# A transformer layer with expert retrieval in fp32: 160 instead of 144 tokens by gathered rows, low halves on GpSimd, rotary scores in fp32r

## The chip, the core and the metric

One core of a Trainium2 chip runs the whole layer. The metric is device time in microseconds (us) of one execution, lower is better; the time given is the median of several runs. The engines are PE (TensorE matmul), PEld (its weight loads), DVE (VectorE), ACT (ScalarE), POOL (GpSimd) and SP (SyncE, which only issues DMAs).

## What is computed

512 tokens of width 2048 go through latent attention (8 heads, 128 plain and 64 rotary columns), a gating unit, an output projection, a retrieval over 16384 one-neuron experts, a per-layer gate and a last RMSNorm. The part that takes most of the time is the retrieval:

```
q  = a @ w_q ; s1, s2 = scores against two sets of 128 keys, per head
experts, gates = the best 16 of the pair sums, per token and head (8 heads: 128 picks per token)
h   = sum over d of u_exp[experts] * a
out = sum over picks of gates * gelu(h) * v_exp[experts]
```

Rotary attention adds `q_rope . k_rope` (64 columns) to `q_nope . k_nope` (128 columns) before the softmax.

## The kernel before

Activations lie transposed, channels on partitions and tokens along the free axis. Large products are made of three fp32r matmuls each (`three`): an fp32 number is split into a high half (a copy rounded to fp32r) and a low half (the number minus its high half), and high by high, high by low and low by high are added in PSUM. Weights come in tiles of 1 MB through a stream of slots. For slot n, SP loads `raw`, ACT writes `wH` (L588), DVE writes `wL` = raw - wH (L986, called `lo`), and PE multiplies. SP, ACT, DVE, POOL and PE each work through a fixed list in order and wait on semaphores, so whatever stands behind a waiting instruction in the same list waits as well.

The retrieval serves two sets of tokens in two ways.

**Dense columns.** The first 368 tokens (`TD`) are multiplied with all 16384 experts. In the u stretch 128 slots ("chunks" of 128 experts) give the neurons' inputs: 16 products of `three`, 48 matmuls of 368 columns in each. 32 of these slots lie in the routing of the heads (with 16 slots of 512 columns for the queries), 96 follow. In the v stretch 128 slots of 48 matmuls go back to the 2048 channels. In v slot v (v = 8g+q) the chunk v+8 is got ready: SP loads `pre_in` and `gate_in`, POOL multiplies them (L551), ACT makes the high half `actH` (L841, `weight_hi`), DVE the low half `actL` (L1502, `weight_lo`); PE reads both from the next group of eight slots on.

**Gathered tokens.** The last 128 tokens stand one on a partition. For each of their 128 picks POOL gathers a row of u and v per partition (L543, 16 KB by 128 partitions, 2.1 MB), DVE makes the dot product (`dot`, L1476), ACT gelu and gate (`weigh_pick`, L858 and L862), DVE adds the weighted v row (`add_row`, L1485). 16 more tokens (`BT`) are spread over 8 sets of partitions, so that all their 128 picks take `B_PICKS` = 16 further gathers: 144 in all. A pick is two steps, dot and add. 60 picks are dealt over the chunks 36 to 118 of the u stretch on three row buffers (between two gathers POOL scatters gates with four indirect DMAs, L524), 4 over the last eight chunks on one buffer, and 80 over 118 v slots (`v_step`), on the two row buffers `rows3` and `rows4`. The gather of pick j+2 waits for the add of pick j.

In a v slot the lists read:

- ACT: `wH` of the next slot; for each dot of this slot `weigh_pick`; then `weight_hi`.
- DVE: accumulate; the slot's first step; `lo` of the next slot; its second step, if any; accumulate; `weight_lo`.
- POOL: multiply chunk v+8; then, for each add of this slot, the gather of two picks on.

The retrieval's last part and the rest of the layer stay on PE too. In the attention, 32 items (8 heads by 4 query blocks) each take an fp32 matmul over the plain columns (L1840), an fp32 matmul over the 64 rotary columns (L1841), a mask matmul (L1842), transposes and the product with the values.

Of the kernel before, what the change touches and what calls it, by code (L numbers as in the profile page):

```python
# [35 lines left out]
BT = 16  # L36
# [4 lines left out]
PARTS = SETS // HEADS  # L41
A_PICKS = HEADS * TOPK
B_PICKS = TOPK // PARTS
# [109 lines left out]
def trunk_layer(nc, a, stream, out, gates_dram, pre_dram):  # L153
# [22 lines left out]

    aH = at("aH", [KD, T], R, A0)
# [72 lines left out]
    gates_b = at("gates_b", [B_PICKS], F, C0 + 12 * KB + 640)  # L250
    dots_b = at("dots_b", [B_PICKS], F, C0 + 12 * KB + 704)
    pick_wb = at("pick_wb", [B_PICKS], F, C0 + 12 * KB + 768)
# [4 lines left out]
    pick_w = at("pick_w", [P], F, C0 + 13 * KB + 512)  # L257
    ones = at("ones", [P], F, C0 + 14 * KB)
# [12 lines left out]
    with ctx:  # L271
        ps = ctx.enter_context(nc.psum_tensor("ps", [P, 8, 512], F))

        def sem(name):
            return ctx.enter_context(nc.semaphore(name))
# [19 lines left out]
        kv_copied = sem("kv_copied")  # L295
        score_done, nbias_ready, exp_done, p_ready = sem("score_done"), sem("nbias_ready"), sem("exp_done"), sem("p_ready")
# [59 lines left out]
        def _(sp):  # L356
# [104 lines left out]
        def _(pool):  # L461
# [43 lines left out]
            for i in range(4):  # L505
                pool.dma_start(hT[:, 4 * i:4 * i + 4, :], a["x"][:, 4 * i:4 * i + 4, :]).then_inc(x_again, 16)
# [68 lines left out]
        def _(act):  # L575
# [398 lines left out]
        def _(dve):  # L974
# [242 lines left out]
            for n in range(ITEMS + 1):  # L1217
# [8 lines left out]
                if n >= 1:  # L1226
# [5 lines left out]
                    V.tensor_scalar(prob[m % 2][:, 0:w], prob[m % 2][:, 0:w], rinv[:, m:m + 1], None, ALU.mult).then_inc(p_ready, 1)  # L1232
                if n >= NT + 4 and n % NT == 0 or n == ITEMS:
# [275 lines left out]
            for c in range(ROUTE_U + 2, KEYS):  # L1509
                scale_chunk(c - 1, (c - 1) % 2, CUM[nu + c - 1])  # L1510
                steps = range(u_step(c), u_step(c + 1))
                for o in steps[0:1]:
                    pick_step(o)
# [3 lines left out]
                if c >= KEYS - GROUP:  # L1517
                    weight_lo(c - KEYS + GROUP, c - KEYS + GROUP, 0, pre_in[c % 2])
# [10 lines left out]
            def v_end(g, q, b, m, i):  # L1529
                c = GROUP * (g + 1) + q  # L1530
# [3 lines left out]
                weight_lo(c, q, 1 - b, pre_in[q % 2])  # L1534
# [124 lines left out]
        def _(pe):  # L1659
# [168 lines left out]
            pe.wait_ge(rope_ready, 5)  # L1828
            pe.wait_ge(mean_ready, NORMS["sgu"] + 1)
            ITEMS = HEADS * NT  # L1830
            for n in range(ITEMS + 3):
                if n < ITEMS:
# [5 lines left out]
                    r = slice(64 * (h % 2), 64 * (h % 2) + 64)  # L1838
# [279 lines left out]
```

## Time and profile before

| | us |
|---|---|
| median of 3 runs | 3081.89 (3081.18 to 3085.0) |
| profiled execution | 3090.69 |
| its span | 3089.0 |

The span was profiled once; 1.7 us of the profiled execution lie outside it. On the page PE is busy for 3052.4 us (99%), DVE for 2228.9 (72%), ACT for 1061.4 (34%), POOL for 1211.7 (39%). A PE row's length holds the pipeline's depth and says little of its rate: the distance from one start to the next is the rate. Of the 40 slices of the span, the DMA engines are at 9 tenths or more in most of those from 1080 to 2780 us.

### The profile page before, as it was taken

How to read it: one execution, taken by the hardware profiler on the slowest of the kernel's cores; microseconds unless marked ns; L12 is line 12 of the kernel's file. 1: busy time of each engine (PE TensorE's matmuls, PEld its weight loads, DVE VectorE, ACT ScalarE, POOL GpSimd, SP SyncE). 2: the span in 40 equal slices, each digit the busy share in tenths (PEclk: the TensorE clock that was granted, in tenths of full speed). 3: DMA queues.
4: the chain of work that ended last, by engine and by line, in shares of the span. 5: the costliest groups of instructions: out<-in, count | busy, mean ns of one | idle time of the engine just before them, and what ended most of it. 6: DMA issues, size and time to landing. Idle time of an engine off the chain costs nothing. (4 is left out here: it accounts for less than half of the span.)

```text
span 3089.0 us, 42590 instructions
## 1 busy us (share of the span) xinstructions
PE 3052.4 (99%) x16888; PEld 2862.8 (93%) x16888; DVE 2228.9 (72%) x2944; ACT 1061.4 (34%) x1328; POOL 1211.7 (39%) x702
## 2 busy tenths in 40 slices
PE   9999999999999999999999999999999999999998
PEld 7888668899999999999999999999999999999887
DVE  5465553478778767777777658888888888997545
ACT  5234442333332433333333333333333333334422
POOL 1010000008888888788887112332333232440000
PEclk9999899999999999999999999999999999999999
DMA  8472202235545599999999779989889999994222
GB/s 296 165 245 90 96 36 101 95 119 126 136 119 137 128 359 347 337 352 347 357 313 373 269 298 356 356 356 361 352 348 360 358 356 366 350 347 162 96 95 95
DMA packets 191487, 768.59 MB, mean 249 GB/s; under 512 B 68608, under 2 KB 121872, under 8 KB 129392
## 3 DMA queue, kind: packets, MB, share of 16 engines
q1 hardware_dynamic: 90768, 407.45, 36.0%
q0 software_dynamic: 81632, 335.12, 30.3%
q10 hardware_dynamic: 18944, 24.14, 2.3%
q8 instruction: 85, 1.39, 0.2%
q14 instruction: 58, 0.48, 0.0%
HBM read 714.00 MB, written 52.62 MB: 248 GB/s over the span
## 5 line engine op out<-in xcount | busy, mean ns | idle before, releaser
L1664 PE MATMUL ps<-aH,wH 128*128 128x368 f32 (+2 forms) x3088 | 1076.2, 349 | 7.5 <-DVE wL L986 5.4
L1665 PE MATMUL ps<-aL,wH 128*128 128x368 f32 (+2 forms) x3088 | 1072.3, 347 | 0.0
L1666 PE MATMUL ps<-aH,wL 128*128 128x368 f32 (+2 forms) x3088 | 1072.2, 347 | 0.0
L588 ACT ACTIVATE wH<-raw 128x2048 fp32r<-128x2048 f32 x333 | 637.9, 1915 | 1013.3 <-PE ps L1666 845.9
L986 DVE TENSOR_TENSOR wL<-raw,wH 128x2048 fp32r<-128x2048 f32 x333 | 783.8, 2354 | 193.2 <-ACT wH L588 192.3
L524 POOL DMA_INDIRECT gates<-gates_r,idx_d x384 | 746.8, 1945 | 369.6 <-DVE gates_r L1387 237.6
L1664 PE MATMUL ps<-actH,wH 128*128 128x368 f32 x2048 | 673.6, 329 | 3.3 <-DVE wL L986 3.3
L1665 PE MATMUL ps<-actL,wH 128*128 128x368 f32 x2048 | 673.5, 329 | 0.0
L1666 PE MATMUL ps<-actH,wL 128*128 128x368 f32 x2048 | 673.5, 329 | 0.0
L1664 PEld LDWEIGHTS ps<-aH,wH 128*128 128x128 f32 x3088 | 580.7, 188 | 47.3 <-DVE wL L986 6.4
L1665 PEld LDWEIGHTS ps<-aL,wH 128*128 128x128 f32 x3088 | 580.8, 188 | 38.7 <-issue 1.0
L1666 PEld LDWEIGHTS ps<-aH,wL 128*128 128x128 f32 x3088 | 580.7, 188 | 38.5
L1664 PEld LDWEIGHTS ps<-actH,wH 128*128 128x128 f32 x2048 | 384.7, 188 | 3.6 <-DVE wL L986 3.6
L1666 PEld LDWEIGHTS ps<-actH,wL 128*128 128x128 f32 x2048 | 384.7, 188 | 0.0
L1665 PEld LDWEIGHTS ps<-actL,wH 128*128 128x128 f32 x2048 | 384.6, 188 | 0.0
L551 POOL TENSOR_TENSOR pre_in<-pre_in,gate_in 128x368 f32<-128x368 f32 x128 | 184.6, 1442 | 413.1 <-DMA gate_in<-gates 410.9
L543 POOL DMA_INDIRECT rows<-uv_rows,idx_s x128 | 214.7, 1677 | 335.5 <-DVE hT L1485 296.2
L1476 DVE SCALAR_TENSOR_TENSOR rows<-rows,ps 128x2048 f32<-128x2048 f32 x128 | 291.7, 2279 | 19.3 <-DMA rows<-uv_rows,idx_s 18.9
L1485 DVE SCALAR_TENSOR_TENSOR hT<-rows,pick_w,hT 128x2048 f32<-128x2048 f32 x128 | 300.2, 2346 | 0.0
L1396 DVE TENSOR_TENSOR ut<-ps,rstd 128x368 f32<-128x368 f32 x128 | 69.2, 541 | 211.8 <-PE ps L1666 188.2
L1507 DVE TENSOR_TENSOR hT<-hT,ps 128x368 f32<-128x368 f32 x256 | 135.5, 531 | 89.1 <-PE ps L1666 88.5
L858 ACT ACTIVATE dots<-dots 128x1 f32<-128x1 f32 x128 | 26.0, 203 | 259.2 <-DVE rows L1476 244.0
(260 smaller groups left out, 1981.2 us busy)
## 6 DMA issues: line engine op xcount, KB each, us to landing
raw<-s_pu SPq DMA_DIRECT2D x128, 1024.0 KB
raw<-s_pv SPq DMA_DIRECT2D x128, 1024.0 KB
gates<-zeros POOLq DMA_DIRECT2D x23, 1024.0 KB, 8.3
pre<-ut ACTq DMA_DIRECT2D x128, 184.0 KB
pre_in<-pre SPq DMA_DIRECT2D x128, 184.0 KB
gate_in<-gates SPq DMA_DIRECT2D x128, 184.0 KB
raw<-s_out SPq DMA_DIRECT2D x16, 1024.0 KB
raw<-s_pq SPq DMA_DIRECT2D x16, 1024.0 KB
```

The lines of the kernel that those rows point to most:

```text
L524: pool.indirect_dma_start(out=gates_flat, out_offset=bass.IndirectOffsetOnAxis(ap=idx_d[0:m, t, c:c + 1], axis=0), in_=gates_r[0:m, t, c:c ...
L543: pool.indirect_dma_start(out=rows[ROW_AT[j]][:, :, :].rearrange("p a d -> p (a d)"), out_offset=None, in_=a["uv_rows"], in_offset=bass.In ...
L551: nc.gpsimd.tensor_tensor(pre_in[b][:, :], pre_in[b][:, :], gate_in[b][:, :], ALU.mult).then_inc(act_gated, 1)
L588: A(wH[parity][:, :], raw[at_n][:, :], ACT.Copy).then_inc(hi_ready, 1)
L986: V.tensor_tensor(wL[parity][:, :], src[:, :], wH[parity][:, :].bitcast(F), ALU.subtract).then_inc(lo_ready, 1)
L1396: V.tensor_tensor(ut[b][:, :], ps[:, 6 + b, 0:TD], rstd[:, 0:TD], ALU.mult).then_inc(chunk_scaled, 1)
L1476: V.scalar_tensor_tensor(r3, r3, 1.0, act_of, ALU.mult, ALU.mult, accum_out=d).then_inc(dot_done, 1)
L1485: V.scalar_tensor_tensor(hT[:, :, TA:T], v3, pick_w[:, j:j + 1], hT[:, :, TA:T], ALU.mult, ALU.add).then_inc(pick_done, 1)
L1507: V.tensor_tensor(h, h, ps[:, 4 + k % 4, 0:TD], ALU.add).then_inc(h_acc, 1)
L1664: mm(out, wh, xh, start=start, stop=False)
L1665: mm(out, wh, xl, start=False, stop=False)
L1666: return mm(out, wl, xh, start=False, stop=stop)
```

## The change

- `BT` goes from 16 to 32: 160 tokens are gathered and 352 columns stay dense (`TD`). The 32 tokens lie in 4 sets, which take `B_PICKS` = 32 gathers: 160 picks, of which 96 are dealt over the same 118 v slots.
- The low half of the activations, `actL`, is made by POOL, in `apply_gates` behind its multiply and behind a wait for ACT's high half, and no longer by DVE. POOL's gathers stand behind it.
- In the last eight chunks of the u stretch, ACT makes the high half before it weighs a pick, and each of the four last picks gets its dot in one slot and its add in the next.
- SP loads late chunk 2 before value tiles 4 to 6.
- The rotary parts of q and k are split in high and low halves (`ropeQ`, `ropeKH`, `ropeKL`; ACT copies, DVE subtracts), and the rotary scores are two fp32r matmuls: one over 128 rows (q high and q low against k high, doubled) and one over 64 rows (q high against k low). The product of low by low is left out. Eight DVE scalings of `mixT` move into the attention's items, and three of four reloads of x wait for the last score.

```diff
-BT = 16
+BT = 32
 SETS = P // BT
-PARTS = SETS // HEADS
-B_PICKS = TOPK // PARTS
+B_PICKS = A_PICKS // SETS
...
     if c > KEYS - GROUP:
-        return 2 * (U_PICKS - LATE + min((c - KEYS + GROUP + 1) // 2, LATE))
+        return 2 * (U_PICKS - LATE) + min(c - KEYS + GROUP, 2 * LATE)
...
             load_late_chunk(1)
+            load_late_chunk(2)
             load_value(4)
             load_value(5)
-            for v in range(2, KEYS - GROUP):
+            load_value(6)
+            for v in range(3, KEYS - GROUP):
...
                 nc.gpsimd.tensor_tensor(pre_in[b][:, :], pre_in[b][:, :], gate_in[b][:, :], ALU.mult).then_inc(act_gated, 1)
+                pool.wait_ge(act_whi, c + 1)
+                nc.gpsimd.tensor_tensor(actL[c // GROUP % 2][:, c % GROUP, 0:TD], pre_in[b][:, :],
+                                        actH[c // GROUP % 2][:, c % GROUP, 0:TD].bitcast(F), ALU.subtract).then_inc(act_wlo, 1)
...
+                    if s == 1:
+                        r = head_rows(m)
+                        act.wait_ge(rope_ready, 2 + m // 2)
+                        A(ropeQ[r, m, :], qT[r, 8 + m // 2, :], ACT.Copy).then_inc(rope_hi, 1)
...
                 u_beat(c, c % 2, nu + c, 0)
+                weight_hi(c - KEYS + GROUP, c - KEYS + GROUP, 0, pre_in[c % 2])
                 for o in range(u_step(c), u_step(c + 1)):
                     if o % 2 == 0:
                         weigh_pick(o // 2)
-                weight_hi(c - KEYS + GROUP, c - KEYS + GROUP, 0, pre_in[c % 2])
...
+                if 5 <= n + 4 < HEADS:
+                    rope_low(n + 4)
+                if 0 <= n - 10 < SGU_TILES:
+                    g = n - 10
+                    V.scalar_tensor_tensor(mixT[:, 8 + g, :], mixT[:, 8 + g, :], gain("sgu", g), rstdB[:, :],
+                                           ALU.mult, ALU.mult).then_inc(sgu_scaled, 1)
...
-            def weight_lo(c, j, b, src):
-                dve.wait_ge(act_whi, c + 1)
-                V.tensor_tensor(actL[b][:, j, 0:TD], src[:, :], actH[b][:, j, 0:TD].bitcast(F), ALU.subtract).then_inc(act_wlo, 1)
...
-                weight_lo(c, q, 1 - b, pre_in[q % 2])
...
-                    mm(o, qT[r, 8 + h // 2, t], krT[r, 0:w], start=False, stop=False)
+                    if qt == 0:
+                        pe.wait_ge(rope_lo, 2 + h)
+                    mm(o, ropeQ[:, h, t], ropeKH[:, 0:w], start=False, stop=False)
+                    mm(o, ropeQ[r, h, t], ropeKL[r, 0:w], start=False, stop=False)
```

POOL's list in the v stretch, before (`pre_in` is the multiply, `rows` a gather):

```order
L551 TENSOR_TENSOR pre_in_132<-pre_in_132,gate_in_134 128x368
L543 DMA rows_86<-uv_rows,idx_s 128x4096
L551 TENSOR_TENSOR pre_in_131<-pre_in_131,gate_in_133 128x368
L543 DMA rows_87<-uv_rows,idx_s 128x4096
L551 TENSOR_TENSOR pre_in_132<-pre_in_132,gate_in_134 128x368
```

and of the change:

```order
L561 TENSOR_TENSOR pre_in_134<-pre_in_134,gate_in_136 128x352
L563 TENSOR_TENSOR actL_85<-pre_in_134,actH_83 128x352
L553 DMA rows_90<-uv_rows,idx_s 128x4096
L561 TENSOR_TENSOR pre_in_135<-pre_in_135,gate_in_137 128x352
L563 TENSOR_TENSOR actL_85<-pre_in_135,actH_83 128x352
L553 DMA rows_89<-uv_rows,idx_s 128x4096
```

The subtraction that reads `actH` has come between each multiply and the gather behind it. On ACT, in the same place of the change, the instruction that writes `actH` stands behind the weighing of the slot's dot, as it did before:

```order
L601 ACTIVATE wH_71<-raw_69 128x2048
L879 ACTIVATE dots<-dots 128x1
L883 ACTIVATE pick_w<-dots,gates_r 128x1
L862 ACTIVATE actH_83<-pre_in_135 128x352
L601 ACTIVATE wH_72<-raw_70 128x2048
```

Nothing moved on ACT there. What is new is that POOL now waits for the fourth row. On PE, the first two items of the attention before:

```order
L1840 MATMUL ps<-kT,qT 128x128
L1841 MATMUL ps<-krT,qT 128x128
L1842 MATMUL ps<-causalR,identR 128x128
L1840 MATMUL ps<-kT,qT 128x256
L1841 MATMUL ps<-krT,qT 128x256
```

and of the change:

```order
L1868 MATMUL ps<-kT,qT 128x128
L1871 MATMUL ps<-ropeKH,ropeQ 128x128
L1872 MATMUL ps<-ropeKL,ropeQ 128x128
L1873 MATMUL ps<-causalR,identR 128x128
L1868 MATMUL ps<-kT,qT 128x256
L1871 MATMUL ps<-ropeKH,ropeQ 128x256
L1872 MATMUL ps<-ropeKL,ropeQ 128x256
```

Each rotary matmul has become two, of another type.

## Rows read from the trace of the kernel before

**Rows 1.** Windows: busy us (x instructions) by engine, PE clock, DMA share, GB/s.
```profile
700.00:1000.00 300.00, 300.00 (x1657) 281.25 (x1657) 245.21 (x778) 96.88 (x97) 258.07 (x127) 1.00 0.51 130
1100.00:1700.00 600.00, 600.00 (x3602) 600.00 (x3601) 451.31 (x315) 201.47 (x260) 487.24 (x269) 1.00 0.98 348
1800.00:1880.00 80.00, 72.20 (x412) 71.29 (x411) 50.38 (x41) 26.98 (x32) 15.98 (x13) 0.96 0.79 308
1880.00:2700.00 820.00, 820.00 (x4922) 820.00 (x4921) 712.22 (x620) 273.12 (x343) 273.03 (x173) 1.00 0.91 356
```

**Rows 2.** Timeline of PE (start, us, operation): 512 columns, then 368 columns.
```profile
307.93 0.39 PE L1666 MATMUL ps<-cqH,wL 128*128 128x512 f32 x1
...
308.61 0.39 PE L1666 MATMUL ps<-cqH,wL 128*128 128x512 f32 x1
...
1499.92 0.33 PE L1664 MATMUL ps<-aH,wH 128*128 128x368 f32 x1
...
1501.92 0.33 PE L1664 MATMUL ps<-aH,wH 128*128 128x368 f32 x1
```

**Rows 3.** Groups by line and form: the 368 column matmuls of u and of v.
```profile
L1664 PE MATMUL ps<-aH,wH 128*128 128x368 f32 x2048 | 675.2, 330 | 4.5 <-DVE wL L986 4.5
L1664 PE MATMUL ps<-actH,wH 128*128 128x368 f32 x2048 | 673.6, 329 | 3.3 <-DVE wL L986 3.3
```

**Rows 4.** Timeline of the attention on PE: rotary matmul and the mask matmul behind it.
```profile
381.78 1.12 PE L1841 MATMUL ps<-krT,qT 64*128 64x512 f32 x2
382.83 0.33 PE L1842 MATMUL ps<-causalR,identR 128*128 128x128 f32 x1
...
383.78 0.49 PE L1841 MATMUL ps<-krT,qT 64*128 64x128 f32 x2
384.19 0.33 PE L1842 MATMUL ps<-causalR,identR 128*128 128x128 f32 x1
```

**Rows 5.** Timeline of POOL in the u stretch: one gather to the next.
```profile
1403.06 1.43 POOL L543 DMA_INDIRECT rows<-uv_rows,idx_s  x1 [0.30 <-issue]
...
1413.26 1.00 POOL L543 DMA_INDIRECT rows<-uv_rows,idx_s  x1 [0.30 <-issue]
```

**Rows 6.** Timeline of a v slot with an add and a dot: DVE.
```profile
2306.80 2.34 DVE L1485 SCALAR_TENSOR_TENSOR hT<-rows,pick_w,hT 128x2048 f32<-128x2048 f32 x1
2309.06 2.28 DVE L986 TENSOR_TENSOR wL<-raw,wH 128x2048 fp32r<-128x2048 f32 x1
2311.26 2.28 DVE L1476 SCALAR_TENSOR_TENSOR rows<-rows,ps 128x2048 f32<-128x2048 f32 x1
```

**Rows 7.** Timeline of the same slot: ACT, then POOL.
```profile
2306.40 1.92 ACT L588 ACTIVATE wH<-raw 128x2048 fp32r<-128x2048 f32 x1 [4.35 <-PE ps L1666]
2313.59 0.20 ACT L858 ACTIVATE dots<-dots 128x1 f32<-128x1 f32 x1 [5.26 <-DVE rows L1476]
...
2314.02 0.49 ACT L841 ACTIVATE actH<-pre_in 128x368 fp32r<-128x368 f32 x1
...
2309.07 3.11 POOL L551 TENSOR_TENSOR pre_in<-pre_in,gate_in 128x368 f32<-128x368 f32 x1 [8.99 <-DMA gate_in<-gates]
2312.34 0.96 POOL L543 DMA_INDIRECT rows<-uv_rows,idx_s  x1 [0.15 <-issue]
...
2318.07 2.78 POOL L543 DMA_INDIRECT rows<-uv_rows,idx_s  x1 [3.75 <-DVE hT L1485]
```

**Rows 8.** Timeline of DVE: the dots for which those two gathers are made.
```profile
2323.13 2.29 DVE L1476 SCALAR_TENSOR_TENSOR rows<-rows,ps 128x2048 f32<-128x2048 f32 x1 [0.25 <-DMA rows<-uv_rows,idx_s]
...
2331.93 2.29 DVE L1476 SCALAR_TENSOR_TENSOR rows<-rows,ps 128x2048 f32<-128x2048 f32 x1 [0.69 <-DMA rows<-uv_rows,idx_s]
```

**Rows 9.** Timeline before the v stretch: a gather (POOL) and its dot (DVE).
```profile
1792.38 1.02 POOL L543 DMA_INDIRECT rows<-uv_rows,idx_s  x1 [8.24 <-DVE hT L1485]
...
1801.69 2.29 DVE L1476 SCALAR_TENSOR_TENSOR rows<-rows,ps 128x2048 f32<-128x2048 f32 x1 [2.53 <-DMA rows<-uv_rows,idx_s]
```

**Rows 10.** Windows, columns as in the first group: five us of the v stretch.
```profile
2220.00:2225.00 5.00, 5.00 (x32) 5.00 (x31) 5.00 (x4) 1.51 (x2) 2.14 (x1) 1.00 1.05 440
```

More of the change, by code:

```diff
@@ L175, in trunk_layer @@
     freq = at("freq", [2], F, H0 + 30 * KB + 800)
+    ropeQ = at("ropeQ", [HEADS, T], R, H0)
+    ropeKH = at("ropeKH", [T], R, H0 + 16 * KB)
+    ropeKL = at("ropeKL", [T], R, H0 + 18 * KB)
     aH = at("aH", [KD, T], R, A0)
@@ L249, in trunk_layer @@
     idx_b = at("idx_b", [B_PICKS], U32, C0 + 12 * KB + 576)
-    gates_b = at("gates_b", [B_PICKS], F, C0 + 12 * KB + 640)
-    dots_b = at("dots_b", [B_PICKS], F, C0 + 12 * KB + 704)
-    pick_wb = at("pick_wb", [B_PICKS], F, C0 + 12 * KB + 768)
+    gates_b = at("gates_b", [B_PICKS], F, C0 + 12 * KB + 704)
     sel = at("sel", [BT], F, C0 + 12 * KB + 832)
@@ L257, in trunk_layer @@
     pick_w = at("pick_w", [P], F, C0 + 13 * KB + 512)
+    dots_b, pick_wb = dots[:, 0:B_PICKS], pick_w[:, 0:B_PICKS]
     ones = at("ones", [P], F, C0 + 14 * KB)
@@ L295, in trunk_layer @@
         kv_copied = sem("kv_copied")
+        rope_hi, rope_lo = sem("rope_hi"), sem("rope_lo")
         score_done, nbias_ready, exp_done, p_ready = sem("score_done"), sem("nbias_ready"), sem("exp_done"), sem("p_ready")
@@ L334, in rstd_of, with head_rows @@
             return {"cq": rstdL, "ckv": rstdL, "sgu": rstdB}.get(name, rstd)
+        def head_rows(h):
+            return slice(64 * (h % 2), 64 * (h % 2) + 64)
         def gain(name, k):
@@ L504, in _ @@
             pool.wait_ge(act_lo, N_SC["sgu"])
-            for i in range(4):
+            for i in (3, 0, 1, 2):
+                if i == 0:
+                    pool.wait_ge(score_done, HEADS * NT)
                 pool.dma_start(hT[:, 4 * i:4 * i + 4, :], a["x"][:, 4 * i:4 * i + 4, :]).then_inc(x_again, 16)
@@ L720, in _ @@
                     A(dst, ps[:, 4 + m % 4, :], ACT.Copy).then_inc(kv_copied, 1)
+                    if (s, m) == (0, 3):
+                        act.wait_ge(rope_ready, 1)
+                        act.wait_ge(sgu_ready, 8)
+                        A(ropeKH[:, :], krT[:, :], ACT.Copy).then_inc(rope_hi, 1)
+                    if s == 1:
+                        r = head_rows(m)
+                        act.wait_ge(rope_ready, 2 + m // 2)
+                        A(ropeQ[r, m, :], qT[r, 8 + m // 2, :], ACT.Copy).then_inc(rope_hi, 1)
                     if s == 0 and m == 1:
@@ L866, in bring_set @@
             def bring_set(i):
-                h, r = divmod(i, PARTS)
                 dst = slice(i * BT, (i + 1) * BT)
-                src = slice(h * TOPK + r * B_PICKS, h * TOPK + (r + 1) * B_PICKS)
+                src = slice(i * B_PICKS, (i + 1) * B_PICKS)
                 act.dma_start(idx_b[dst, :], idx_e[at_b:P, src]).then_inc(b_loaded, 16)
@@ L1210, in _, with rope_low @@
                 rope(1 + j, qT[:, 8 + j, :], qT[:, 8 + j, :])
-            for g in range(SGU_TILES):
-                V.scalar_tensor_tensor(mixT[:, 8 + g, :], mixT[:, 8 + g, :], gain("sgu", g), rstdB[:, :],
-                                       ALU.mult, ALU.mult).then_inc(sgu_scaled, 1)
+            def rope_low(h):
+                dve.wait_ge(rope_hi, 2 + h)
+                r, other = head_rows(h), head_rows(h + 1)
+                V.tensor_tensor(ropeQ[other, h, :], qT[r, 8 + h // 2, :], ropeQ[r, h, :].bitcast(F), ALU.subtract).then_inc(rope_lo, 1)
+            dve.wait_ge(rope_ready, 5)
+            dve.wait_ge(rope_hi, 1)
+            V.tensor_tensor(ropeKL[:, :], krT[:, :], ropeKH[:, :].bitcast(F), ALU.subtract).then_inc(rope_lo, 1)
+            for h in range(5):
+                rope_low(h)
             lo(S0["out"], 0)
@@ L1511, in _ @@
                 steps = range(u_step(c), u_step(c + 1))
-                for o in steps[0:1]:
+                late_dot = c >= KEYS - GROUP and len(steps) == 1 and steps[0] % 2 == 0
+                for o in steps[0:0 if late_dot else 1]:
                     pick_step(o)
@@ L1516, in _ @@
                     pick_step(o)
-                if c >= KEYS - GROUP:
-                    weight_lo(c - KEYS + GROUP, c - KEYS + GROUP, 0, pre_in[c % 2])
+                if late_dot:
+                    pick_step(steps[0])
             def v_begin(g, q, m, i):
```

4 lines of the change are left out of this document (1 added, 3 removed).

## The prediction

> **What bounds the kernel now.** I read the windows first. In the u stretch (1100 to 1700 us) and in the v stretch (1880 to 2700) PE is busy all the time, at full clock [rows 1], so the start-to-start distance of its matmuls is the price of the work. Twelve starts of 368 columns take 2.00 us, 0.1667 us each; three of 512 take 0.68 us, 0.227 each [rows 2]. That is about 0.417 ns per column on top of some 13 ns. A slot of 48 such matmuls takes 8.00 us. But the next limits are close. In the v stretch the DMA engines are at 0.91 and DVE is busy 712 of 820 us; in the u stretch the DMA engines are at 0.98 and POOL is busy 487 of 600 us [rows 1]. Then I read one v slot in the timelines of DVE, ACT and POOL, because the change puts a wait on POOL in front of the gathers: a gather issued at 2312.34 is waited for by its dot until 2323.13, and one issued at 2318.07 until 2331.93 [rows 7, 8]. Both dots came a little before their rows. So the gathers already run without slack, while PE never feels it.
>
> **Fewer columns.** 2048 matmuls of u and 2048 of v, each on three lines, are 12288 of 368 columns [rows 3]. 352 columns cost 0.160 us by the slope above, a slot 7.68 us. 12288 x 6.67 ns = **-81.9 us**, as long as PE stays the bound. Of it 118 x 0.32 = 37.8 us lie in the v slots that carry picks.
>
> **Sixteen more gathers.** They are 96 picks on 118 v slots where 80 were: 0.81 a slot for 0.68. Bytes per slot go from 1.05 (raw) + 0.38 (chunk) + 0.68 x 2.10 = 2.85 MB (356 GB/s x 8.0 us, as in [rows 1]) to 1.05 + 0.36 + 0.81 x 2.10 = 3.12 MB. At equal cost per byte the DMA engines need 0.91 x 3.12 / 2.85 x 8.0 = 7.97 us a slot, 0.3 us more than PE. DVE's work per slot: 712 / 820 x 8.0 = 6.95 us, less 0.45 for the low half, plus 0.136 picks of 4.5 us (add 2.26, dot 2.28) = 7.1 of 7.68 us: 93%, still inside.
>
> **The low half on POOL.** In `apply_gates` POOL now waits for `actH` of the same chunk, and the gather is queued behind. ACT writes `actH` only after it weighed the slot's dot. This costs nothing in a slot with a dot then an add, or with one step. It does in a slot with an **add, then a dot**. Take the slot that starts at 2306.40 [rows 6, 7]: the add ends at +2.7, `wL` at +4.9, the dot at +7.1, `actH` at +8.1. Before, the gather that the add had freed was issued at +5.9, ahead of `actH`. Now POOL subtracts until +9.1 (a POOL operation of this size takes 1 us when DVE does not hold it up) and gathers then. The time L from issue to dot is 10.8 us in the first pair of [rows 7, 8], 13.9 in the second, whose issue fell beside DVE's `wL`, and 9.3 in [rows 9], with less traffic. I take 10.8: once PE stalls there is less traffic than now, but more POOL work meets `wL`.
>
> With 192 steps dealt over 118 slots, 36 slots are of the kind add-dot (20 before), and 14 times two of them stand in a row. Such a pair runs like this, with B and C its slots and D and E the next:
> - B: gather at B+9.1, row usable at B+19.9, which is C+12.2. The dot wants it at C+4.9.
> - C: the dot ends at C+14.5, `actH` at C+15.5. POOL subtracts and issues the next gather at C+16.5, although its buffer was free at C+2.7. ACT writes the next `wH` until C+17.4, DVE its `wL` until C+19.6. PE wanted it at C+15.4: **4.3 us stall**.
> - E begins at C+19.7. Its dot waits for C+16.5+10.8 = E+7.6, ends at E+9.9, `wL` behind it at E+12.1, wanted at E+7.7: **4.5 us stall**.
>
> 8.8 us a pair. An add-dot slot alone (8 of them, with an add slot behind it) makes the dot two slots on start at +4.5 instead of +0.5; its `wL` ends at +9.0: 1.3 us. Sum: 14 x 8.8 + 8 x 1.3 = **+134 us**. With L = 9.3 the same steps give 5.7 and 0 us, sum +80; with L = 13.9 they give 14.5 and 4.4, sum +238. That DVE is rid of 0.45 us a slot does not help, because it is idle in those waits. The clock could add to it: after the idle time around 1800 to 1880 the mean granted clock is 0.96 [rows 1], which is full speed with short pieces at 1.2 GHz; I leave that in the range.
>
> In this slot the POOL multiply took 3.11 us, and it overlaps DVE's `wL` (2309.06 to 2311.34) [rows 6, 7]. The Trainium skill says on its page "GPSIMD Engine Reference", section Specifications, that GpSimd shares its SBUF interfaces with VectorE and contends with DVE instructions that have two SBUF inputs. The trace agrees here, since `wL` has two; by that rule the second POOL operation of a slot would at times take some 3 us as well, and the gather come 2 us later than I reckon.
>
> **Rotary scores.** The fp32 matmul of 512 columns holds PE for 1.05 us, that of 128 for 0.41 [rows 4]; a head with four widths in between takes about 2.9 us. Two fp32r matmuls of 512 cost 2 x 0.227, of 128 2 x 0.067: 1.2 us a head. 8 x 1.7 = 14 us. Against it stand low halves and scalings in DVE's list inside the items. I take **-11 us**, bounds -14 and -5.
>
> **Last picks and late chunks.** Between 1800 and 1880 PE lost 7.8 us idle and 0.04 x 80 = 3.2 us of clock [rows 1]. The single row buffer was the cause: gather at 1792.38, dot at 1801.69 with DVE waiting 2.5 us [rows 9]. With dot and add in different slots the gather has about a slot and a half. **-9 us**, bounds -11 and 0.
>
> **u stretch.** POOL's round of a gather and four scatters takes 10.2 us [rows 5]; 60 picks over 82 slots of 7.68 want one every 10.5 us: it just fits. DMA at 0.98 [rows 1] would be at 1.02. **+6 us**, bounds 0 and +13. The head stretch has DVE at 245 and POOL at 258 of 300 us [rows 1] and keeps its gain.
>
> **Sum.** -81.9 + 134 - 11 - 9 + 6 = **+38 us**. The profiled span of 3089.0 us would become 3127; the median of the runs lies 9 us below the profiled execution, so it would go from 3081.9 to **3120 us**.
>
> **Rivals.**
> - *DMA bound, the wait on POOL absorbed* (if a gather is served within its slack): v slots of 8.0 us, so the 37.8 us are lost and nothing more. -81.9 + 37.8 - 14 = -58: 3024 us. For it: share 0.91 now. Against it: dots already wait [rows 8], and the gather comes 3.2 us later still.
> - *PE stays the bound everywhere* : -81.9 - 14 = -96: 2986 us. It would need the DMA engines to do 3.12 MB in 7.68 us, 406 GB/s; they do 440 for five us [rows 10], but 356 on the mean.
> - *A ceiling of the memory rate.* If the 356 GB/s of the v stretch [rows 1] are all that can be had over long times, a slot takes 3.12 / 0.356 = 8.76 us: 118 x 1.08 - 81.9 - 14 = +31: 3113 us, slower than before even without POOL's wait; it decides once a slot needs more than 356 x 8.0 us = 2.85 MB. Against it stand the 440 GB/s of [rows 10]. The Trainium skill, page "DMA: Bandwidth & Descriptors", section "Where 436 GB/s comes from", gives about 358 GB/s of HBM for each core as what binds, though the section before it says that this is so with both cores of a pair at work.
>
> **How the numbers follow.** POOL's wait decides: 0.65, with 3066 (L = 9.3) to beyond 3180 around its 3120; a tenth of it lies at or under the time before. DMA bound: 0.17. PE bound: 0.10. Memory rate: 0.08. I leave out the PE bound case and the end over 3180: **3020 to 3180**. A measurement of this kernel tells 0.2% from no change; by that, faster 0.17 + 0.10 + 0.04 = 0.31, same 0.05, slower 0.64.
>
> **What the changed kernel's profile would show.** Starts of 352 column matmuls 0.160 us apart. In the v stretch PE waits for `wL` in sums over 80 us, in pieces of 3 to 5 us, two slots in a row; DVE's dots wait for rows, 5 us and more; POOL's subtraction waits for `actH`. DMA share under 0.95 there. If instead the share is 1.0 and the slots are an even 8 us, the DMA rival holds; if PE shows no waits, the second one does. What would make me wrong most easily is L: a gather that takes 8 us when the queues are idle cuts the stalls by more than half.

## The result, and the profile of the changed kernel

The changed kernel takes **3321.74 us** (median; 3313.01 to 3325.27), the kernel before 3081.53 in the same comparison. The ratio is 1.077 (95% interval 1.076 to 1.079): 240 us slower. The direction was forecast, the size was not: 3120 us, at most 3180. The profiled execution has a span of 3323.5 us, against 3089.0 before.

The page: engines, then PE, its clock and the DMA share in 40 slices.

```profile
PE 3042.5 (92%) x16888; PEld 2849.7 (86%) x16888; DVE 2272.6 (68%) x2873; ACT 1063.3 (32%) x1369; POOL 1422.4 (43%) x845
...
PE   9999999999999999999999787878896968788998
...
PEclk9999999999999999999999888988998989899999
DMA  8462132345556999999988777777887878684222
```

Up to slice 22 (some 1830 us) PE is full and its clock high. Then come fifteen slices with gaps in both: the v stretch. The window 1880 to 2700, to hold against the last row of [rows 1] (columns: span, PE, weight load, DVE, ACT, POOL, granted clock, DMA share, GB/s):

```profile
1880.00:2700.00 820.00, 657.50 (x3732) 648.54 (x3731) 573.22 (x429) 209.45 (x286) 348.23 (x222) 0.89 0.79 299
```

PE is busy 657.5 us of 820 where it was busy all the time, at a clock of 0.89. The DMA engines have fallen from 0.91 to 0.79, DVE from 712 to 573 us. Nothing is busier but POOL, and POOL only for 348 us: the engines wait for each other. For whom, the groups of the page tell (the first answers to the second row of [rows 3]; last columns: idle time ahead of the group, and its releaser):

```profile
L1693 PE MATMUL ps<-actH,wH 128*128 128x352 f32 x2048 | 700.1, 342 | 241.2 <-DVE wL L1006 241.1
...
L563 POOL TENSOR_TENSOR actL<-pre_in,actH 128x352 fp32r<-128x352 f32 x128 | 259.4, 2027 | 592.8 <-ACT actH L862 592.8
L1510 DVE SCALAR_TENSOR_TENSOR rows<-rows,ps 128x2048 f32<-128x2048 f32 x128 | 292.2, 2283 | 272.0 <-DMA rows<-uv_rows,idx_s 271.3
```

PE waits 241 us for `wL`, where 3.3 us stood before; DVE, which makes `wL`, waits 271 us for gathered rows (this group is of the whole kernel and of the first 128 picks: 218 us of it lie in the v stretch, where the dots of the 32 spread tokens wait another 112); POOL, which issues the gathers, stands 593 us at its subtraction and waits for `actH`. `actH` itself stands behind the weighing of the dot. That is the ring of the forecast, with all four members.

Where the 234.5 us of span went, from the starts of each stage's matmuls (us):

| stretch | before | after | difference |
|---|---|---|---|
| start to attention | 338.0 | 338.5 | +0.5 |
| attention | 83.9 | 70.4 | -13.5 |
| attention to first u chunk | 215.1 | 213.7 | -1.4 |
| u, first 32 chunks (head stretch) | 425.3 | 415.5 | -9.8 |
| u, the other 96, to the first v slot | 774.7 | 747.9 | -26.8 |
| v, first two slots | 16.0 | 15.4 | -0.6 |
| **v, 118 slots with picks** | **949.1** | **1236.1** | **+287.0** |
| rest | 276.4 | 275.6 | -0.8 |

The stretches end with the start of the last matmul. All of the loss lies in the 118 v slots; every other stretch gains or stays. In them the matmuls would need 118 x 7.68 = 906.2 us, and 329.9 us come on top. PE's idle time is 241.2 us of them (3.3 before). Some 7.5 us are idle time that the rows hide: a row is 0.32 us long while the next start is due after 0.16, so each of the 45 stalls looks 0.16 us shorter than it is. The last 81 us are clock: in 262.8 us of this stretch PE was granted the lower of its two levels, 1.2 GHz (3.4 us before), and in 161 us of these it had matmuls to do, which it started at half the rate.

### The profile page after: what moved, and what is told of

It is laid out like the page before. It is cut to its first block and busy times, and to the rows that moved or that the text cites. A ratio compares the mean times of both kernels' runs of the same rounds, so it can differ in the third digit from the quotient of the medians.

```text
span 3323.5 us, 42713 instructions
## 1 busy us (share of the span) xinstructions
PE 3042.5 (92%) x16888; PEld 2849.7 (86%) x16888; DVE 2272.6 (68%) x2873; ACT 1063.3 (32%) x1369; POOL 1422.4 (43%) x845
## 5 line engine op out<-in xcount | busy, mean ns | idle before, releaser
L1693 PE MATMUL ps<-aH,wH 128*128 128x352 f32 (+2 forms) x3088 | 1063.9, 345 | 10.3 <-DVE wL L1006 8.2
L1695 PE MATMUL ps<-aH,wL 128*128 128x352 f32 (+2 forms) x3088 | 1060.1, 343 | 0.0
L1694 PE MATMUL ps<-aL,wH 128*128 128x352 f32 (+2 forms) x3088 | 1059.9, 343 | 0.0
L1693 PE MATMUL ps<-actH,wH 128*128 128x352 f32 x2048 | 700.1, 342 | 241.2 <-DVE wL L1006 241.1
L1694 PE MATMUL ps<-actL,wH 128*128 128x352 f32 x2048 | 691.7, 338 | 0.0
L1695 PE MATMUL ps<-actH,wL 128*128 128x352 f32 x2048 | 690.5, 337 | 0.0
L1693 PEld LDWEIGHTS ps<-actH,wH 128*128 128x128 f32 x2048 | 412.7, 202 | 255.4 <-DVE wL L1006 255.3
L1693 PEld LDWEIGHTS ps<-aH,wH 128*128 128x128 f32 x3088 | 581.8, 188 | 52.0 <-DVE wL L1006 10.8
L563 POOL TENSOR_TENSOR actL<-pre_in,actH 128x352 fp32r<-128x352 f32 x128 | 259.4, 2027 | 592.8 <-ACT actH L862 592.8
L1510 DVE SCALAR_TENSOR_TENSOR rows<-rows,b_tok 128x2048 f32<-128x2048 f32 x32 | 89.1, 2784 | 112.0 <-DMA rows<-uv_rows,idx_b 112.0
L1430 DVE TENSOR_TENSOR ut<-ps,rstd 128x352 f32<-128x352 f32 x128 | 67.0, 523 | 144.1 <-PE ps L1695 104.7
```

Of the source, the lines that this page charges most:

```text
L563: nc.gpsimd.tensor_tensor(actL[c // GROUP % 2][:, c % GROUP, 0:TD], pre_in[b][:, :], actH[c // GROUP % 2][:, c % GROUP, 0:TD].bitcast(F), ...
L1430: V.tensor_tensor(ut[b][:, :], ps[:, 6 + b, 0:TD], rstd[:, 0:TD], ALU.mult).then_inc(chunk_scaled, 1)
L1510: V.scalar_tensor_tensor(r3, r3, 1.0, act_of, ALU.mult, ALU.mult, accum_out=d).then_inc(dot_done, 1)
L1693: mm(out, wh, xh, start=start, stop=False)
L1694: mm(out, wh, xl, start=False, stop=False)
L1695: return mm(out, wl, xh, start=False, stop=stop)
```

## One pair of slots, read row by row

The forecast rested on pairs of add-dot slots, B and C, then D and E. Here is one of the changed kernel, B starting at 1915.2. DVE (start, us, operation; in brackets idle time and releaser):

```profile
1920.05 2.28 DVE L1510 SCALAR_TENSOR_TENSOR rows<-rows,ps 128x2048 f32<-128x2048 f32 x1
...
1923.32 2.35 DVE L1519 SCALAR_TENSOR_TENSOR hT<-rows,pick_w,hT 128x2048 f32<-128x2048 f32 x1
1925.58 3.04 DVE L1006 TENSOR_TENSOR wL<-raw,wH 128x2048 fp32r<-128x2048 f32 x1
1940.03 2.29 DVE L1510 SCALAR_TENSOR_TENSOR rows<-rows,ps 128x2048 f32<-128x2048 f32 x1 [11.40 <-DMA rows<-uv_rows,idx_s]
...
1943.10 2.34 DVE L1519 SCALAR_TENSOR_TENSOR hT<-rows,pick_w,hT 128x2048 f32<-128x2048 f32 x1
1945.37 3.01 DVE L1006 TENSOR_TENSOR wL<-raw,wH 128x2048 fp32r<-128x2048 f32 x1
...
1958.64 2.29 DVE L1510 SCALAR_TENSOR_TENSOR rows<-rows,ps 128x2048 f32<-128x2048 f32 x1 [9.40 <-DMA rows<-uv_rows,idx_s]
```

ACT, then POOL, in the same stretch:

```profile
1922.81 0.48 ACT L862 ACTIVATE actH<-pre_in 128x352 fp32r<-128x352 f32 x1
...
1942.36 0.20 ACT L879 ACTIVATE dots<-dots 128x1 f32<-128x1 f32 x1 [17.26 <-DVE rows L1510]
```

```profile
1923.37 3.11 POOL L563 TENSOR_TENSOR actL<-pre_in,actH 128x352 fp32r<-128x352 f32 x1 [8.59 <-ACT actH L862]
1926.62 2.85 POOL L553 DMA_INDIRECT rows<-uv_rows,idx_s  x1
1943.35 2.88 POOL L563 TENSOR_TENSOR actL<-pre_in,actH 128x352 fp32r<-128x352 f32 x1 [12.91 <-ACT actH L862]
1946.38 2.83 POOL L553 DMA_INDIRECT rows<-uv_rows,idx_s  x1 [0.15 <-issue]
```

And PE:

```profile
1948.43 0.66 PE L1693 MATMUL ps<-actH,wH 128*128 128x352 f32 x1 [10.12 <-DVE wL L1006]
...
1963.19 0.66 PE L1693 MATMUL ps<-actH,wH 128*128 128x352 f32 x1 [4.18 <-DVE wL L1006]
```

Read it from the left. B's dot ends at 1922.3, which is B+7.1, and `actH` at B+8.1: both to the tenth as reckoned. From there the reckoning was short three times. (1) POOL's subtraction starts with DVE's add (1923.32) and takes 3.11 us, not 1.0: the gather is issued at B+11.4 instead of B+9.1. (2) The gather now falls beside `wL`; its issue takes 2.85 us, and 1940.03 - 1926.62 = 13.4 us pass until the dot, not 10.8. (3) The `wL` for which PE waits takes 3.01 us (at 1945.37), not 2.28. The first two make the dot 2.3 + 2.6 = 4.9 us later, the third adds 0.8; 4.3 us of stall were reckoned, 4.3 + 5.7 = 10.0 would follow, and 10.12 are there. The second stall was reckoned at 4.5 us and is 4.18, but only because two errors cancel: E begins at 1948.43 and its dot at E+10.2 instead of E+7.6, so its `wL` is 2.7 us later than reckoned; PE, at the lower clock, is 2.9 us later too before it wants it.

This pair is one of the dearer. Read in the same way, the stalls of all 14 pairs add up to 187.5 us, 13.4 a pair (8.4 to 15.2), those of the eight lone add-dot slots to 44.6 us, 5.6 each, and 9 us lie elsewhere. In one pair the first stall is short, and it tells what the collisions are worth. There DVE's add began only at 2375.67 and its `wL` at 2379.30, so that POOL's subtraction met neither and the gather's issue was over before `wL`:

```profile
2374.19 0.95 POOL L563 TENSOR_TENSOR actL<-pre_in,actH 128x352 fp32r<-128x352 f32 x1 [2.43 <-ACT actH L862]
2375.28 0.96 POOL L553 DMA_INDIRECT rows<-uv_rows,idx_s  x1
```
```profile
2385.68 2.29 DVE L1510 SCALAR_TENSOR_TENSOR rows<-rows,ps 128x2048 f32<-128x2048 f32 x1 [4.09 <-DMA rows<-uv_rows,idx_s]
```
```profile
2394.08 0.43 PE L1693 MATMUL ps<-actH,wH 128*128 128x352 f32 x1 [3.53 <-DVE wL L1006]
```

The subtraction takes 0.95 us, the gather is issued 2.1 us after the dot's end, its own dot comes 10.4 us later, and the stall is 3.53 us, where 4.3 were reckoned and the other 13 pairs have 7.1 to 10.1. So the reckoning held, near enough, where these collisions did not happen, and that was once in 14.

Windows of the pair at 1915.2 show the clock, and that it prolongs work that waits for nothing:

```profile
1920.00:1938.30 18.30, 18.30 (x114) 18.02 (x112) 8.52 (x7) 2.69 (x4) 6.90 (x3) 1.00 0.70 256
1938.30:1948.43 10.13, 0.01 (x1) 0.00 (x0) 8.40 (x7) 2.69 (x4) 4.93 (x2) 0.61 0.11 34
1948.43:1959.00 10.57, 10.57 (x48) 10.29 (x48) 1.17 (x3) 2.30 (x2) 4.58 (x5) 0.73 0.93 371
```

Ten us without a matmul, and the 48 matmuls behind take 10.57 us instead of 7.68. The subtraction beside the add, and the gather's issue beside `wL`, are what was slow. The rule of the Trainium skill that I cited ("GPSIMD Engine Reference", section Specifications: GpSimd contends with DVE instructions that have two SBUF inputs) agrees with each of these collisions: the add and `wL` both have two. I had named its price and then left it out of the sum.

## The experiments

Each is compared with the kernel before on the same chip (3082 to 3083 us). The columns "118 slots" are from one profiled execution each: length of the v slots with picks, PE's idle time in them, and the time at the lower clock; 7.68 us a slot would be 906 (8.00 us, 944, where 368 columns are left).

| kernel, and its short name | median, us (range) | ratio (95%) | 118 slots | idle | low clock | a slot |
|---|---|---|---|---|---|---|
| before | 3081.5 | 1 | 949.1 | 3.3 | 3.4 | 8.04 |
| changed | 3321.7 (3313-3325) | 1.077 (1.076-1.079) | 1236.1 | 241.2 | 262.8 | 10.48 |
| e1: low half on DVE | 3073.4 (3060-3077) | 0.996 (0.994-0.997) | 991.1 | 51.3 | 44.4 | 8.40 |
| e2: before, low half on POOL | 3138.0 (3136-3150) | 1.018 (1.016-1.019) | 1007.1 | 39.2 | 41.8 | 8.53 |
| e3: gather first | 3068.7 (3059-3076) | 0.995 (0.993-0.997) | 986.0 | 52.5 | 27.3 | 8.36 |
| e4: ACT's order | 3086.1 (3079-3095) | 1.001 (1.000-1.003) | 994.6 | 56.8 | 44.4 | 8.43 |
| e5: both orders | 3057.3 (3052-3064) | 0.993 (0.991-0.994) | 969.0 | 42.3 | 17.1 | 8.21 |
| e6: BT = 16, low half on DVE | 3067.4 (3065-3070) | 0.995 (0.994-0.997) | 944.0 | 0 | 0 | 8.00 |
| e7: whole picks | 3077.2 (3065-3096) | 0.999 (0.997-1.001) | 997.4 | 59.3 | 44.4 | 8.45 |
| e8: three row buffers | 3033.7 (3030-3049) | 0.986 (0.983-0.989) | 948.2 | 25.5 | 17.1 | 8.04 |
| e9: three row buffers, low half on DVE | 3030.2 (3028-3031) | 0.982 (0.981-0.984) | 947.5 | 25.1 | 6.8 | 8.03 |
| e10: before, gather first | 3084.0 (3077-3088) | 1.000 (0.999-1.001) | 947.1 | 2.3 | 0 | 8.03 |

My theory: the low half's place on POOL, ahead of the gather and behind the wait for `actH`. The rivals: the 96 picks by themselves (the DMA engines, or a ceiling of the rate), and POOL's added work on the shared interfaces, wherever it stands.

### e1. The low half back on DVE

```diff
                 nc.gpsimd.tensor_tensor(pre_in[b][:, :], pre_in[b][:, :], gate_in[b][:, :], ALU.mult).then_inc(act_gated, 1)
-                pool.wait_ge(act_whi, c + 1)
-                nc.gpsimd.tensor_tensor(actL[c // GROUP % 2][:, c % GROUP, 0:TD], pre_in[b][:, :],
-                                        actH[c // GROUP % 2][:, c % GROUP, 0:TD].bitcast(F), ALU.subtract).then_inc(act_wlo, 1)
...
+            def weight_lo(c, j, b, src):
+                dve.wait_ge(act_whi, c + 1)
+                V.tensor_tensor(actL[b][:, j, 0:TD], src[:, :], actH[b][:, j, 0:TD].bitcast(F), ALU.subtract).then_inc(act_wlo, 1)
...
                 accumulate(2 * q, CUM[m + q - 1] + 4 * GROUP * i + 1)
+                weight_lo(c, q, 1 - b, pre_in[q % 2])
```

> The change with the low half back on VectorE, all else as changed (160 tokens gathered). Theory 'POOL's wait': the wait in front of the gathers is the cause, so the 118 v slots with picks shrink from 1236 us to what the DMA engines allow, about 8.0 us each (944 to 960), with few stalls and the clock at 1.0: 3020 to 3060 us. Rival 'the 16 further gathers': it is their traffic and VectorE work that stall the slots; VectorE even gets 0.45 us more per slot, so the time stays over 3250 us.

3073 us: 248 us of the loss are gone with this one edit, so the low half on POOL is the cause. But 3073 is above the range that I had given. The window:

```profile
1880.00:2700.00 820.00, 780.07 (x4722) 770.90 (x4722) 730.91 (x633) 263.46 (x356) 279.19 (x178) 0.98 0.95 374
```

40 us are still lost in it. The 96 picks alone cost something that my sum did not have: 991 us for 118 slots where 906 are needed and the DMA engines, by my estimate, would need 941.

### e2. The kernel before, with its low half on POOL

```diff
                 nc.gpsimd.tensor_tensor(pre_in[b][:, :], pre_in[b][:, :], gate_in[b][:, :], ALU.mult).then_inc(act_gated, 1)
+                pool.wait_ge(act_whi, c + 1)
+                nc.gpsimd.tensor_tensor(actL[c // GROUP % 2][:, c % GROUP, 0:TD], pre_in[b][:, :],
+                                        actH[c // GROUP % 2][:, c % GROUP, 0:TD].bitcast(F), ALU.subtract).then_inc(act_wlo, 1)
...
-                weight_lo(c, q, 1 - b, pre_in[q % 2])
```

> The kernel before with one part of the change alone: the low half on POOL (144 tokens gathered). Theory 'POOL's wait': 20 slots of add then dot are delayed, none twice in a row but each followed by a stall of some 5 us, on top the clock: 8.8 us a slot for 8.0, so +100 to +150 us: 3180 to 3230 us. Rival 'the 16 further gathers': without them nothing stalls: 3080 us.

3138 us, +55, less than expected. With 80 picks there are 20 add-dot slots, not 36. In the v slots the edit costs 58 us in the profiled execution, which was the slowest of the four (3149.5). In the change, the 96 picks alone are 991.1 - 906.2 = 85 us above PE's own time, and both together 330: more than the two added up (58 + 85 = 143). What could join them is taken up in e7.

### e3. The gather ahead of the low half

Nothing is taken from POOL; two entries of its list change places.

```diff
+            def low_half(c, b):
+                pool.wait_ge(act_whi, c + 1)
+                nc.gpsimd.tensor_tensor(actL[c // GROUP % 2][:, c % GROUP, 0:TD], pre_in[b][:, :],
+                                        actH[c // GROUP % 2][:, c % GROUP, 0:TD].bitcast(F), ALU.subtract).then_inc(act_wlo, 1)
...
                 nc.gpsimd.tensor_tensor(pre_in[b][:, :], pre_in[b][:, :], gate_in[b][:, :], ALU.mult).then_inc(act_gated, 1)
-                pool.wait_ge(act_whi, c + 1)
-                nc.gpsimd.tensor_tensor(actL[c // GROUP % 2][:, c % GROUP, 0:TD], pre_in[b][:, :],
-                                        actH[c // GROUP % 2][:, c % GROUP, 0:TD].bitcast(F), ALU.subtract).then_inc(act_wlo, 1)
+                if c < GROUP:
+                    low_half(c, b)
...
                             gather(o // 2 + 2)
+                    low_half(GROUP * (g + 1) + q, q % 2)
```

> The change with two entries of POOL's list exchanged in the v slots: the slot's gather stands before the low half, not behind it. Same work, same engines, same memory traffic. Theory 'POOL's wait': 8.1 to 8.3 us a slot, 3040 to 3090 us. Rival 'shared ports' (POOL's second operation and VectorE's two-input operations hold each other up): the operations still meet, so at least half of the loss stays: over 3180 us. Rival 'further gathers': over 3250 us.

3069 us, as good as with the low half on DVE. The same operations on the same engine, 253 us apart by their order. The whole loss is in the place. The waits of the change, from 1850 to 2750 us (engine, what, waited for: us in all, times, longest), and those of this kernel:

```profile
POOL actL L563 <- ACT actH L862: 408.5, 86, 12.9
DVE rows L1510 <- DMA rows<-uv_rows,idx_s: 217.7, 29, 11.4
...
PE ps L1693 <- DVE wL L1006: 175.4, 31, 10.1
```

```profile
POOL actL L560 <- ACT actH L868: 120.3, 54, 7.5
...
DVE rows L1516 <- DMA rows<-uv_rows,idx_s: 65.5, 37, 5.0
...
PE ps L1699 <- DVE wL L1012: 51.5, 35, 4.5
```

POOL still waits 120 us for `actH`, but the slot's own gather no longer stands behind that wait. The dots' waits for these rows are down from 218 to 66 us, in pieces of 1.8 us instead of 7.5.

### e4. ACT's order turned instead

```diff
                 if not tail:
+                    weight_hi(GROUP * (g + 1) + q, q, 1 - b, pre_in[q % 2])
                     for o in range(v_step(g, q), v_step(g, q + 1)):
...
                             weigh_pick(o // 2)
-                    weight_hi(GROUP * (g + 1) + q, q, 1 - b, pre_in[q % 2])
```

> The change with ScalarE's list altered in the v slots: the high half is made before the dot is weighed, so that POOL's low half no longer waits for the dot; POOL's list as changed. Theory 'POOL's wait': the link from the dot to the next gather is cut, the queueing behind the subtraction stays; 8.6 to 8.8 us a slot, 3100 to 3150 us. Rival 'shared ports' or 'further gathers': over 3250 us.

3086 us, below the range expected. POOL's list is the change's, but `actH` no longer stands behind the dot's weighing: this opens the ring at another place and is worth 236 us, more than I had given it. So neither order is bad alone; it takes both for the ring.

### e5. Both orders

The two edits above together.

> The change with both edits of the runs before: POOL's gather ahead of its low half, and ScalarE's high half ahead of weighing the dot. Theory 'POOL's wait' has nothing left to cut but the last queueing: 8.1 to 8.3 us a slot, 3030 to 3060 us. What then remains over 7.68 us a slot is the gathers' own.

3057 us; they do not add up, since either opens the ring, but together they leave less: 969 us for the 118 slots.

### e6. BT = 16, with the low half on DVE

This leaves of the change only the rotary scores, the last picks and late chunks, with 368 columns as before (`BT = 32` becomes `BT = 16`, and the edit of the first experiment).

> The change with 144 tokens gathered (80 picks in the v slots) and the low half on VectorE: only the rotary scores, the last picks and the load order are left of it. Expected: v slots of 8.00 us as before, attention 84 to 70 us, no idle PE between the stretches: 3055 to 3065 us. If the rest of the loss in the v slots came from the new load order instead of the further gathers, the v stretch would be over 960 us here too.

3067 us, just above the range. From the 32nd u chunk to the first v slot it takes 769.9 us, against 774.7: **4.8 us** for the last picks. The 118 slots take 944.0 us, just what PE needs. So of the change only the sixteen gathers and the low half's place touch the v slots.

### e7. Picks dealt whole

The change as it is, with POOL's wait in place, but the dot and add of a pick always in the same slot, so that no slot has an add and then a dot.

```diff
-    return 2 * U_PICKS + max(0, GROUP * g + q - FIRST_SLOT) * 2 * (PICKS - U_PICKS) // slots
+    return 2 * U_PICKS + max(0, GROUP * g + q - FIRST_SLOT) * (PICKS - U_PICKS) // slots * 2
```

> The change, POOL's and ScalarE's lists in the changed order, but picks dealt whole: 96 of the 118 v slots have a dot and then an add, the others nothing, so that no slot has an add and then a dot. Theory 'pairs of add-dot slots': POOL's wait is never behind a later pick's dot, the long stalls (9 to 10 us) vanish; but a gather issued at the slot's end (+8) has only 8 us to the dot two slots on where picks follow each other, so stalls of 2 to 5 us stay: 8.3 to 8.8 us a slot, 3060 to 3130 us. If POOL's wait costs in every slot alike, over 3250 us.

3077 us: one number of the dealing, and 245 us are back. The wait is still there, and often:

```profile
POOL actL L563 <- ACT actH L862: 221.6, 107, 7.0
```

107 times, 222 us in all, but none of the 10 us pieces: I take it that this is so because a slot now adds after its dot, so that the buffer for the next gather comes free late anyway and the wait is mostly over by then. So the wait needs the add-dot slots to hurt, as reckoned. With more picks there are more of them, 36 for 20, and they stand in a row. That is a part of what joined the two causes in e2, but not all of it: all the idle time in the slots of e2 is 39 us, some 2 us for each of its 20 lone add-dot slots, and the eight lone ones of the change cost 5.6 us each. What makes a lone one dearer with 96 picks, the steps in the slots around it or the fuller DMA engines, no run separates.

### e8. A third row buffer in the v stretch

With the ring opened, the slots still took 8.2 to 8.4 us where 7.68 was PE's and 7.97 the estimate for the DMA engines. Either the two row buffers leave too little time for a gather, or the DMA rate is less than I think. This takes the version with both orders, gives the picks of v a third buffer and issues each gather one pick earlier; the room comes from the value tiles' third and fourth `raw` buffer, and SP's order of loads in the v stretch changes with it.

```diff
-    _at = _j % 3 if _j < U_PICKS - LATE else 2 if _j < U_PICKS else 3 + _j % 2
+    _at = _j % 3 if _j < U_PICKS - LATE else 2 if _j < U_PICKS else 3 + _j % 3
...
-    raw += [at(f"raw{2 + i}", [2048], F, A0 + (32 + 8 * i) * KB) for i in range(2)]
...
-                        if o % 2 == 1 and o // 2 + 2 < PICKS:
-                            gather(o // 2 + 2)
+                        if o % 2 == 1 and o // 2 + 3 < PICKS:
+                            gather(o // 2 + 3)
```

> The kernel of both orders with three row buffers in the v slots instead of two, and two raw buffers instead of four (the room of the other two). A gather then has a pick's time more. Theory 'latency of the gather': 7.7 to 7.9 us a slot, 2995 to 3025 us. Theory 'DMA rate': the slot stays at 8.0 us or over, the DMA share goes to 1.0: 3030 us or more. Should raw tiles come late with two buffers, PE waits for them instead: over 3050 us.

3034 us, at the edge between the two expectations. The slots say more:

```profile
1880.00:2700.00 820.00, 800.97 (x4935) 794.54 (x4934) 761.95 (x559) 280.87 (x375) 432.89 (x291) 1.00 0.98 392
```

DMA share 0.98, 392 GB/s over 820 us, 8.04 us a slot. With the third buffer 0.17 of the 0.24 us over the DMA engines' estimate are gone (8.21 to 8.04, for 7.97), so I put them down to the time that a gather had. At this share the DMA engines are close to full, and ACT waits for raw tiles; that these now have two buffers instead of four may have a part in that wait, which no run separates:

```profile
ACT wH L593 <- DMA raw<-s_pv: 97.4, 35, 5.9
```

### e9. The same buffers, the low half on DVE

The first experiment with these buffers: no POOL work added at all.

> Three row buffers and two raw buffers as in the run before, but the low half on VectorE. Theory 'DMA rate' (what is left over 7.68 us a slot in the three-buffer kernel is memory traffic): about the same, 3025 to 3045 us. Rival 'shared ports' (POOL's second operation still costs VectorE time there): under 3020 us. VectorE gets 0.45 us more work per slot, to 95%; if that is felt, over 3045 us.

3030 us, 948 us for the 118 slots as in e8. It is the best of all versions, 1.8% below the kernel before. POOL's subtraction, in a harmless place, makes no difference that can be told: 3.5 us between the medians, with ranges that overlap, and 0.7 us in the slots (the two kernels differ in ACT's order as well).

### e10. The kernel before, with gather first

```diff
                 nc.gpsimd.tensor_tensor(pre_in[b][:, :], pre_in[b][:, :], gate_in[b][:, :], ALU.mult).then_inc(act_gated, 1)
+                if c < GROUP:
+                    low_half(c, b)
...
                             gather(o // 2 + 2)
+                    low_half(GROUP * (g + 1) + q, q % 2)
...
-                weight_lo(c, q, 1 - b, pre_in[q % 2])
```

> The kernel before with the low half on POOL (as in the run with that part alone) but behind the slot's gathers instead of ahead of them. Theory 'POOL's wait': the place in the list was the whole cost of that run (3138 us), so 3078 to 3090 us. Rival 'shared ports': the second POOL operation costs wherever it stands, over 3110 us.

3084 us, no change that can be told. Against the +55 us of the same work ahead of the gather:

```profile
1880.00:2700.00 820.00, 819.42 (x4917) 819.12 (x4916) 673.59 (x516) 273.44 (x342) 434.91 (x274) 1.00 0.91 357
```

POOL is busy 435 us of 820 here, 162 more than before [rows 1], DVE 39 less, and PE does not feel it. The rival by which POOL's added traffic on the shared interfaces is the cost falls. The collisions are real, and they lengthen the ring where there is one, but on a path with slack they cost nothing.

## The prediction, point by point

- **The bound, the columns.** Right. 352 columns start 0.160 us apart (2289.78 to 2291.70 for twelve, below); the head stretch of 32 slots gained 9.8 us of 32 x 0.32 = 10.2.

```profile
2289.78 0.32 PE L1693 MATMUL ps<-actH,wH 128*128 128x352 f32 x1
...
2291.70 0.32 PE L1693 MATMUL ps<-actH,wH 128*128 128x352 f32 x1
```

- **The low half on POOL: the step that failed.** The mechanism, its members and its place were right, and e3, e4, e7 and e10 show them. The mis-sized term is the +134 us: PE's idle time in the 118 slots grew by 237.9 us. It failed where the prediction says "I take 10.8", with a subtraction that "takes 1 us when DVE does not hold it up". DVE did hold it up. The add-dot slots have 36 gathers. All but one of them were issued 4.1 to 4.3 us after the dot's end, not 2.0, because the subtraction met the add, and the issue itself fell beside `wL` and took some 2.85 us; from issue to dot, L, it took 12.2 us on the mean of the 36, 9.8 to 13.5, not 10.8. In the change the subtraction starts where `actH` ends, which is where DVE's next add starts, so that in such a slot the gather behind it falls on `wL`.

  [Rows 7] had the evidence: the one gather there that was issued beside `wL` took 2.78 us to issue, and its dot came 13.9 us later. It was no single case: in the v stretch of the kernel before, the dots that waited for a gather issued beside `wL` came 13.4 to 14.1 us after it (ten), the others 10.9 to 12.0 (six). So an L over 10.8 was the one to take for these slots, with the 2 us of the other collision on top.

  My own upper case for it is also mis-added: by the steps L counts in both stalls of a pair, so 13.9 gives 8.8 + 2 x 3.1 = 15.0 us a pair, not 14.5, and +245, not +238. That +238 meets the measured 237.9 is luck: L was shorter than in that case, the issue came 2 us later, and at the lower clock PE wanted the second tile later (13.4 us a pair, 5.6 a lone slot).
- **The clock: not in the sum at all.** I left it "in the range", sized by a stretch with 7.8 us of idle time. PE was at the lower level for 262.8 us of the 118 slots, which cost some 81 us. That is most of the 92 us between my upper case (-81.9 + 238 - 11 - 9 + 6 = +142) and the +234.5 of the span. The range was cut at 3180 although the bound L = 13.9 alone gave 3224; the chance of the end that I left out was too small.
- **The sixteen gathers: hidden behind the +134, but not free.** I had them as a rival only, at 7.97 us a slot. With two row buffers the slots took 8.2 to 8.5 us once the long stalls were gone, with three 8.03 at a DMA share of 0.98: the estimate was good, as a bound that this kernel did not reach. The rival "DMA bound" (3024 us) is what e9 comes to: 3030.
- **Memory rate.** Refuted: 356 GB/s was what was asked for. e8 and e9 held 392 and 389 over 820 us. The Trainium skill, page "DMA: Bandwidth & Descriptors", section "Where 436 GB/s comes from", gives some 358 GB/s of HBM for a core as what binds; it did not bind the one core that the program uses, and the measurement decides.
- **Rotary scores.** -11 forecast. The attention shrank by 13.5 us, but before's profile had 17.1 us at the lower clock in it. e2 and e10, with the old rotary scores and none of that, took 76.7 and 76.6 us, the change 70.4: the edit is worth **6.2 us**. From the first to the last start of the scores (before, e2, changed):

```profile
L1840 PE MATMUL ps<-kT,qT x64: 275/486/1061, 338.0 to 421.9; 128*128 128x128 f32 x16, 128*128 128x256 f32 x16, 128*128 128x384 f32 x16, 128*128 128x512 f32 x16
```
```profile
L1835 PE MATMUL ps<-kT,qT x64: 275/458/595, 338.1 to 414.8; 128*128 128x128 f32 x16, 128*128 128x256 f32 x16, 128*128 128x384 f32 x16, 128*128 128x512 f32 x16
```
```profile
L1868 PE MATMUL ps<-kT,qT x64: 275/458/596, 338.5 to 408.9; 128*128 128x128 f32 x16, 128*128 128x256 f32 x16, 128*128 128x384 f32 x16, 128*128 128x512 f32 x16
```

- **Last picks, late chunks.** -9 forecast, -4.8 in e6: half, and inside the bounds.
- **u stretch.** +6 forecast, bounds 0 and +13. The 96 chunks and the last picks should have given 30.7 + 4.8 = 35.5 us and gave 26.8, so some 9 us were lost. PE stood 6.5 us in 1100 to 1700 in the change and not at all in e3, whose lists are the same there. In the seven other kernels with 352 columns the stretch took 742.5 to 745.0 us, 3 to 6 us more than that gain would leave: there the +6 is about right. The change's own 3 to 5 us beyond them are more than the seven differ among themselves (2.5 us) and stay open.
- **What would be seen.** Waits for `wL` over 80 us, two slots in a row; dots waiting over 5 us; POOL's wait for `actH`; DMA under 0.95: all seen. The pieces were to be 3 to 5 us; in the pairs they were 3.5 to 10.

What stays open: why the change with two row buffers and an open ring takes 8.2 us a slot with both orders turned and 8.4 with one, and what makes a lone add-dot slot three times as dear with 96 picks as with 80. Nor was the three-buffer version run with another dealing of the steps.

## What to carry over

An instruction that waits should not stand ahead of a DMA issue on an in-order engine, above all where what it waits for stands behind the consumer of that same DMA: then a ring closes, and its round sets the pace of all engines though none is busy. The cure was the order of two list entries, not less work. When a latency has been measured twice and the two differ, find out what made the longer one long, and ask if the change makes that the rule; and once a sum contains stalls of several us, price the clock behind them as well.

## What the runs showed of the hardware

- After a stall of 10 us PE ran at a granted clock of 0.73 on the mean over the next slot (1948.43 to 1959.00) and took 10.57 us for 48 matmuls that need 7.68. Over the 118 slots the lower clock cost 81 us on top of 241 us of idle time, a third as much again.
- A POOL subtraction of 128x352 in the v stretch of the change took 0.94 to 0.96 us alone (24 of them) and 1.97 to 3.11 us beside a DVE operation with two inputs in SBUF: the add, `wL`, or the dot of a spread token (95). The issue of a gather took 0.96 to 0.98 us alone and up to 2.85 beside one of these; DVE's `wL` was slowed too, from 2.28 to at most 3.04 us.
- From a gather's issue to the dot that waited for it (2.1 MB): before, 13.4 to 14.1 us where the issue met `wL`, 10.9 to 12.0 where it did not; in the change, with the DMA engines less full, 9.8 to 13.5 and 9.2 to 11.2.
- One core held 392 GB/s for 820 us at a DMA share of 0.98.
